# Second attention: two heads per step, with the forget passes and the fp32 scores of both on the two row halves of TensorE

## The reference, cut to what matters

```python
def fox_mixer(xn, w_q, w_o, k, v, c):      # c: cumulative log forget gates, (B, T, H)
    q = (xn @ w_q).reshape(B, T, B_HEADS, HEAD_DIM)
    for i in range(T // BLK):              # BLK = 128
        s = jnp.einsum('bqhd,bkhd->bhqk', q[:, q0:q1], k[:, :q1]) * HEAD_DIM ** -0.5
        s = s + (c_t[:, :, q0:q1, None] - c_t[:, :, None, :q1])
        s = jnp.where(causal, s, NEG)
        p = jax.nn.softmax(s, axis=-1)
        outs.append(jnp.einsum('bhqk,bkhd->bqhd', p, v[:, :q1]))
    return jnp.concatenate(outs, axis=1).reshape(B, T, B_WIDTH) @ w_o
```

## Time and profile before

| | |
|---|---|
| median of 3 runs | 2332.89 us (2332.63 to 2333.86) |
| span of the profiled execution | 2330.7 us |
| TensorE matmul busy | 2212.4 us, 95% of the span |
| second attention, first scores to last values | about 720.1 to 913.6 us |
| of it, with fill between its parts | 720.1 to 893.7 us |

### The profile page before, as it was taken

One profiled execution on the slowest core, in us unless ns is written; L12 is line 12 of the kernel. 1 busy time (PEld: TensorE's weight loads), 2 busy tenths in 40 slices (PEclk: granted clock), 3 DMA queues, 4 the chain that ended last, 5 costly groups with the idle time before them and its releaser, 6 DMA issues.

```text
span 2330.7 us, 34187 instructions
## 1 busy us (share of the span) xinstructions
PE 2212.4 (95%) x14110; PEld 1813.9 (78%) x14110; DVE 1420.4 (61%) x1976; ACT 584.5 (25%) x1199; POOL 1129.2 (48%) x642
## 2 busy tenths in 40 slices
PE   7999899999999999999999998999988978999998
PEld 5877688888877777778788767887888867888886
DVE  6555678667654444667957869687855773721632
ACT  2143322022133222222012132335444222200200
POOL 5711466765744221466666543372400254757654
PEclk9999999999999999999999999999989989999999
DMA  5310223532622110233432551122200111323321
GB/s 176 114 37 19 69 94 118 172 100 92 220 68 68 37 44 21 73 96 109 154 120 98 194 175 37 55 73 74 64 3 3 48 38 55 106 92 99 101 91 63
DMA packets 55769, 201.94 MB, mean 87 GB/s; under 512 B 6560, under 2 KB 6816, under 8 KB 54720
## 3 DMA queue, kind: packets, MB, share of 16 engines
q1 hardware_dynamic: 52272, 187.21, 24.5%
q0 software_dynamic: 1840, 9.60, 1.1%
q10 hardware_dynamic: 1504, 2.95, 0.5%
HBM read 194.76 MB, written 4.19 MB: 85 GB/s over the span
## 4 chain that ended last, share of the span: by engine, by line
PE 86%; DVE 8%; ACT 4%; POOL 1%; issue 1%; DMA 0%; SPq 0%; DVEq 0%; POOLq 0%; ACTq 0%
PE bank L522 65%; PE bank L960 3%; PE bank L988 3%; PE bank L2510 1%; PE bank L975 1%; PE bank L654 1%; PE bank L2774 1%; PE bank L2506 1%; PE bank L964 1%; PE bank L2495 1%; POOL parts_r L503 1%; PE bank L1583 1%; PE bank L1595 1%; PE bank L1395 1%; DVE big L1760 0%
## 5 line engine op out<-in xcount | busy, mean ns | idle before, releaser
L522 PE MATMUL bank<-xn_r,parts_r 128*128 128x512 f32 (+1 forms) x2928 | 917.6, 391 | 32.6 <-DVE mix_r L740 12.7
L522 PE MATMUL bank<-big_r,parts_r 128*128 128x512 f32 x3208 | 929.6, 392 | 2.8 <-POOL parts_r L503 2.4
L497 POOL TENSOR_SCALAR parts_r<-ring 128x1024 fp32r<-128x1024 f32 x293 | 340.0, 1160 | 947.0 <-PE bank L522 936.6
L503 POOL TENSOR_TENSOR parts_r<-ring,parts_r 128x1024 fp32r<-128x1024 f32 x293 | 738.5, 2520 | 24.4
L522 PEld LDWEIGHTS bank<-big_r,parts_r 128*128 128x128 f32 x3208 | 601.3, 189 | 133.5 <-issue 5.6
L522 PEld LDWEIGHTS bank<-xn_r,parts_r 128*128 128x128 f32 x2928 | 553.7, 191 | 151.4 <-issue 27.6
L867 ACT ACTIVATE big<-bank,small 128x512 f32<-128x512 f32 x88 | 68.4, 779 | 411.8 <-DVE big L911 253.1
L896 DVE TENSOR_TENSOR bank<-bank,nb 128x512 f32<-128x512 f32 x88 | 61.3, 699 | 143.5 <-PE bank L522 143.4
L3115 DVE TENSOR_TENSOR big<-big 128x512 f32<-128x512 f32 x32 | 82.7, 2586 | 71.1 <-ACT big_r L3096 71.1
L3041 DVE SCALAR_TENSOR_TENSOR h<-bank,vecs,h 128x512 f32<-128x512 f32 x24 | 17.9, 750 | 173.1 <-PE bank L522 173.1
L533 DVE TENSOR_TENSOR big_r<-big,big_r 128x512 fp32r<-128x512 f32 x76 | 105.7, 1393 | 0.4
(11 more groups left out here) (415 smaller groups left out, 2910.8 us busy)
## 6 DMA issues: line engine op xcount, KB each, us to landing
ring<-weights SPq DMA_DIRECT2D x295, 512.0 KB, 3.5
cst<-mod_w SPq DMA_DIRECT2D x48, 512.0 KB, 3.9
cst<-consts SPq DMA_DIRECT2D x2, 1280.0 KB, 8.4
h<-x SPq DMA_DIRECT2D x8, 256.0 KB, 6.9
h_store<-h POOLq DMA_DIRECT2D x8, 256.0 KB, 2.3
big<-consts POOLq DMA_DIRECT2D x2, 1024.0 KB, 8.2
h<-h_store POOLq DMA_DIRECT2D x1, 2048.0 KB, 9.3
out<-mix SPq DMA_DIRECT2D x8, 256.0 KB, 2.2
```

What stands on the lines that cost most here:

```text
L497: pool.tensor_scalar(rounded(unit_parts(u)[0]), ring[:, u % RING], 1.0, 0.0, ALU.mult, ALU.add)\
L503: pool.tensor_tensor(rounded(lo), ring[:, u % RING], value(hi), ALU.subtract).then_inc(part_ready, 1)
L522: mm = pe.matmul(ps, rounded(w[a]), rounded(x[b]), start=(start and n == 0), stop=(stop and n == 2))
```

## The change

A task now is a pair of heads with a block of queries, 32 in all. TensorE issues the two forget passes first, head 0 on rows 0 to 63 and head 1 on rows 64 to 127, and then both fp32 scores, again on the two halves, into banks 0 and 1. For that `b_sel` and `b_c` hold their rows twice, also 64 partitions higher, and the forget pass has 64 rows instead of 128. Scores run one task ahead instead of two, a piece of fill has two chunks instead of one, and eight chunks are done ahead of the attention instead of six. VectorE writes two more pieces of `b_c`, and takes the third projection before it does. Of a task's two transposes ScalarE copies head 0's and VectorE head 1's. One reciprocal and one `row_out` serve both heads.

```diff
-        sel[h, h] = sel[32 + h, h] = -8.0
+        sel[h, h] = sel[32 + h, h] = sel[HD + h, h] = sel[HD + 32 + h, h] = -8.0
...
-        b_tasks = [(tb, [hd]) for hd in range(B_HEADS) for tb in MIXED]
-        PAIR = 2 * len(MIXED)
+        b_tasks = [(pair, tb) for pair in range(KD) for tb in MIXED]
+        PAIR = len(MIXED)
+        b_S = part(b_work, 4, T).rearrange("p (b g) n -> p b g n", b=2)
...
+        KQ_AHEAD = 2
         def kq_fill(pe, t, half):
-            pair, m = divmod(t + 3, PAIR)
+            pair, m = divmod(t + KQ_AHEAD, PAIR)
             if pair + 1 < KD:
-                kq_part(pe, pair + 1, [(m // 4, 2 * (m % 4) + half)])
+                k = 4 * (m % 2) + 2 * half
+                kq_part(pe, pair + 1, [(m // 2, k), (m // 2, k + 1)])
...
+        def pair_scores(pe, t):
+            pair, tb = b_tasks[t]
+            w = (tb + 1) * P
             if t % PAIR == 0:
+                pe.wait_ge(sem("b_kqt"), 2 * pair + 2)
+            ps = [grab(pe, g, *after("b_masked", 2 * t + g + 1)) for g in range(2)]
+            k_, q_ = kq_slot(0, pair), kq_slot(1, pair)
+            own = slice(tb * P, (tb + 1) * P)
+            for g, r in enumerate(half_rows):
+                pe.matmul(ps[g][:, 0:w], rounded(b_sel[r, 2 * pair + g]), rounded(b_c[r, 0:w]), start=True, stop=False)
+            for g, r in enumerate(half_rows):
+                pe.matmul(ps[g][:, 0:w], b_kq[r, q_, own], b_kq[r, k_, 0:w], start=False, stop=True).then_inc(sem("b_scores"), 1)
...
+        def b_pe(pe):
+            pair_scores(pe, 0)
+            for t in range(b_n + 1):
+                if t + 1 < b_n:
+                    pair_scores(pe, t + 1)
+                kq_fill(pe, t, 0)
+                if t < b_n:
+                    pair_turn(pe, t)
+                kq_fill(pe, t, 1)
+                if t >= 1:
+                    pair_values(pe, t - 1)
...
+        def b_act(act):
+            pair_probs(act, 0)
+            for t in range(b_n):
+                if t + 1 < b_n:
+                    pair_probs(act, t + 1)
+                w = (b_tasks[t][1] + 1) * P
+                act.wait_ge(*after("b_turned", 2 * t + 1))
+                if t >= 2:
+                    act.wait_ge(*after("b_values", t - 1))
+                act.activation(b_PT[t % 2][0][:, 0:w], bank[4][:, 0:w], ACT.Copy).then_inc(sem("b_pt_act"), 1)
...
-            for t in range(-3, 0):
+            for t in range(-KQ_AHEAD, 0):
...
-            for c in range(2):
-                kq_take(dve, c)
+            for i in range(2 + KQ_AHEAD // 2):
+                kq_take(dve, i)
             dve.wait_ge(cst_in, 32)
             c_rows = lambda a, b: rounded(b_c[a:b])
             link(dve, dve.tensor_scalar(c_rows(0, P), cst[:, 0:T], 0.0, None, ALU.mult))
+            dve.tensor_copy(c_rows(HD, HD + B_HEADS), z)
             link(dve, dve.tensor_copy(c_rows(0, B_HEADS), z))
+            dve.tensor_tensor(c_rows(HD + 32, HD + 32 + B_HEADS), z, value(b_c[0:B_HEADS]), ALU.subtract)
             dve.tensor_tensor(c_rows(32, 32 + B_HEADS), z, value(b_c[0:B_HEADS]), ALU.subtract).then_inc(sem("b_c"), 1)
             b_dve(dve)
```

More of the change, by code:

```diff
@@ L338 @@
                ("gd_ss", 3)],
-    "weighted": [("a_values", 16), ("b_values", 64), ("U", 2 * TB), ("gl_o", TB)],
+    "weighted": [("a_values", 16), ("b_values", 32), ("U", 2 * TB), ("gl_o", TB)],
     "rotated": [("conv", 4), ("gl_U", NCH - 1)],
@@ L361 @@
     "pt_dve": [("a_pt_dve", 24), ("b_pt_dve", 32)],
-    "rows": [("a_rows", 16), ("b_rows", 64), ("spec", 2 * TB), ("gl_S", NCH - 1)],
-    "max": [("a_max", 16), ("b_max", 64), ("Y", 2 * TB), ("gl_A", TB)],
+    "rows": [("a_rows", 16), ("b_rows", 32), ("spec", 2 * TB), ("gl_S", NCH - 1)],
+    "max": [("a_max", 16), ("b_max", 32), ("Y", 2 * TB), ("gl_A", TB)],
     "convolved": [("ffn0_conv", 2 * KF), ("ffn1_conv", 2 * KF), ("hy_u", 6), ("gd_conv", 15)],
@@ L935, in build, with attention @@
         MIXED = (0, 2, 3, 1)
-        def attention(st, tasks, G, qT, kT, vT, oT, masks, ring, banks, work, sel=None, due=None, fill=None, take_in=None):
+        def attention(st, tasks, G, qT, kT, vT, oT, masks, ring, banks, work):
             Sb = big[:, work:work + 3 * G * T].rearrange("p (b g n) -> p b g n", b=3, g=G)
@@ L953, in scores @@
                 w = (tb + 1) * P
-                if due:
-                    due(pe, t)
                 for g, hd in enumerate(heads):
@@ L960, in scores @@
                     mm = pe.matmul(ps[:, 0:w], qT[r:r + HD, hd // 2 % ring, tb * P:(tb + 1) * P],
[L961 to L965, removed]
+                                   kT[r:r + HD, hd // 2 % ring, 0:w], start=True, stop=True)
                     mm.then_inc(s("scores"), 1)
@@ L1078, in rows_dve @@
                         row_out(dve, t - 1)
-                    if take_in:
-                        take_in(dve, t)
             return rows_pe, rows_act, rows_dve, n
@@ L1181, in mixa_dve @@
             out_dve(dve, "a", "g01", ("g02", ffn_x, "ffn0_xn"))
-        b_q, b_k = part(0, 2, T), part(2 * T, 2, T)
+        b_kq = part(0, 4, T)
         b_v, b_o = part(4 * T, TB, D), part(4 * T + TB * D, TB, D)
@@ L1187, in build, with kq_slot @@
         b_x, b_xkv = (xn, mix), (part(b_work + 5 * T, KD, T), part(b_work + 5 * T + KD * T, KD, T))
-        b_mask = cst[:, 0:T].rearrange("p (g n) -> p g n", g=1)
+        b_mask = cst[:, 0:T]
         b_sel = cst[:, T:T + B_HEADS * P].rearrange("p (h n) -> p h n", h=B_HEADS)
         b_c = nb[:, 0]
-        b_tasks = [(tb, [hd]) for hd in range(B_HEADS) for tb in MIXED]
-        PAIR = 2 * len(MIXED)
+        b_tasks = [(pair, tb) for pair in range(KD) for tb in MIXED]
+        b_n = len(b_tasks)
+        PAIR = len(MIXED)
         b_oT = (xn, part(0, KD, T))
+        b_S = part(b_work, 4, T).rearrange("p (b g) n -> p b g n", b=2)
+        b_PT = [[big[:, b_work + 4 * T:b_work + 5 * T], nb[:, 1]], [nb[:, 2], nb[:, 3]]]
+        half_rows = [slice(HD * g, HD * (g + 1)) for g in range(2)]
+        def kq_slot(c, pair):
+            return 2 * c + pair % 2
         def kq_part(pe, pair, ks):
@@ L1210, in kq_part, with kq_done @@
                     product_done[u] = after("b_kq", i + 1)
+        KQ_AHEAD = 2
         def kq_fill(pe, t, half):
-            pair, m = divmod(t + 3, PAIR)
+            pair, m = divmod(t + KQ_AHEAD, PAIR)
             if pair + 1 < KD:
-                kq_part(pe, pair + 1, [(m // 4, 2 * (m % 4) + half)])
+                k = 4 * (m % 2) + 2 * half
+                kq_part(pe, pair + 1, [(m // 2, k), (m // 2, k + 1)])
+        def kq_done(t):
+            pair, m = divmod(t + KQ_AHEAD, PAIR)
+            return 2 * (pair + 1) + m // 2 if m % 2 and pair + 1 < KD else None
@@ L1218, in kq_take @@
         def kq_take(dve, i):
+            slot = kq_slot(i % 2, i // 2)
             dve.wait_ge(*after("b_kq", i + 1))
[L1220 to L1228, removed]
-            if t % PAIR == 0:
-                pe.wait_ge(sem("b_kqt"), 2 * (t // PAIR) + 2)
@@ L1232, in build @@
-        b_pe, b_act, b_dve, b_n = attention("b", b_tasks, 1, b_q, b_k, b_v, b_o, b_mask, 2, 2, b_work, sel=(b_sel, b_c),
-                                            due=kq_due, fill=kq_fill, take_in=kq_take_in)
+            if i >= 4:
+                dve.wait_ge(*after("b_scores", 2 * PAIR * (i // 2 - 1)))
+            dve.tensor_tensor(b_kq[:, slot], bank[2 + i % 2][:, :], rstd, ALU.mult).then_inc(sem("b_kqt"), 1)
+        b_stat = lambda t, n: stat[:, 16 * (t % 4) + 2 * n:16 * (t % 4) + 2 * n + 2]
@@ new lines, in pair_turn, with pair_values @@
+        def pair_turn(pe, t):
+            pair, tb = b_tasks[t]
+            for g in range(2):
+                ps = grab(pe, 4 + g, *after("b_pt_dve" if g else "b_pt_act", t + 1))
+                pe.wait_ge(*after("b_probs", 2 * t + g + 1))
+                for kb in range(tb + 1):
+                    mm = pe.transpose(ps[:, kb * P:(kb + 1) * P], b_S[:, t % 2, g, kb * P:(kb + 1) * P], ident)
+                mm.then_inc(sem("b_turned"), 1)
+        def pair_values(pe, t):
+            pair, tb = b_tasks[t]
+            ps = grab(pe, 6 + t % 2, *after("b_rows", t + 1))
+            for g in range(2):
+                pe.wait_ge(*after("b_pt_dve" if g else "b_pt_act", t + 1))
+                for kb in range(tb + 1):
+                    mm = pe.matmul(ps[:, g * HD:(g + 1) * HD], b_PT[t % 2][g][:, kb * P:(kb + 1) * P],
+                                   b_v[:, kb, (2 * pair + g) * HD:(2 * pair + g + 1) * HD], start=(kb == 0), stop=(kb == tb))
+            mm.then_inc(sem("b_values"), 1)
@@ new lines, in b_pe, with pair_probs @@
+        def b_pe(pe):
[9 more added lines that the diff above has]
+                    pair_values(pe, t - 1)
+        def pair_probs(act, t):
+            w = (b_tasks[t][1] + 1) * P
+            act.wait_ge(*after("b_max", t + 1))
+            if t >= 4:
+                act.wait_ge(*after("b_rows", t - 3))
+            for g in range(2):
```

(46 more changed lines are left out.)

4 lines of the change are left out of this document (removed).

## The result

The kernel after takes 2312.99 us in the median of 20 runs, the one before 2333.49 us in 20. The ratio is 0.9919, with a 95% interval of 0.9903 to 0.9935: faster by 19 us (15 to 23), or by 20.5 us if the medians are subtracted. One run in 20 of each kernel, at 2365.8 and 2345.2 us, was slow as a whole (the latter at a mean granted clock of 0.954, the profiled run at 0.972), and the ratio leaves these two out. The forecast was 2310.4, with a range of 2303 to 2320.

What follows compares the result with a forecast made beforehand. The prediction took TensorE's stream to bound the second attention. 31.7 us gained, less 1.9 for the last tasks, 5.8 idle and 1.5 for the clock, gave 22.5: 2332.9 - 22.5 = 2310.4 us, range 2303 to 2320.

Steps and rivals of the forecast that it cites:

- What bounds it: Second attention: TensorE's stream bounds the kernel, busy for all of the 173.6 us that have fill.
- The second head is free: Scores and forget passes: the second head on the other half costs nothing; 3.96 us gained a pair, 31.7 over eight.
- the fixed parts: From score start to fill start in each task: 0.31 us that does not grow with the columns.
- the breaks: Between values and the next scores: some 0.03 us once a task; merging saves 0.12 a pair.
- Strict order: Rival, scores on two halves: MATMULs start first in, first out, costing 8.6 us, so 2319; chance 7%.
- Idle time ahead of the first scores: TensorE waits for b_c behind the third projection and a CAST held by GpSimd: 5.8 us lost.
- The clock: After the idle time ahead of the first scores: about 3 us of work at half speed, 1.5 lost, between 0 and 4.
- The last six tasks: Tasks without fill: waits of 0.2, 0.6 and 1.3 us before transposes, 2.1 in sum, 1.9 lost net.
- with 0.15 for the scaling: Chain from scores to transposes, 512 columns: scaling the maxima counted as 0.15 of about 3.95 us.
- The sum: Whole kernel: 31.7 - 1.9 - 5.8 - 1.5 = 22.5 us gained, giving 2310.4 us.

Runs made afterwards that it cites:

- on one half: Against the kernel after, both heads' forget passes and scores are put on rows 0 to 63: 2333.71 us, ratio 1.0002 to the kernel before.
- head-by-head: Against the kernel after, issue order is forget 0, score 0, forget 1, score 1 instead of both forgets, then both scores: 2312.20 us, ratio 0.9915.
- the later split: Against the kernel after, GpSimd splits the sixth key and query unit only when b_c is written: 2310.92 us, ratio 0.9899.
- the two scalings: Against the kernel after, the scaling of two maxima (128x2) is done as two instructions of 128x1: 2310.66 us, ratio 0.9900.
- all three edits: Against the kernel after: c written before the third projection, scaling as two 128x1, ScalarE's copy ahead of the next exponentials from task 26: 2303.71 us, ratio 0.9859.
- c first: Against the kernel after, VectorE writes c into b_c before it takes the third projection: 2309.80 us, ratio 0.9908.
- extra matmuls: Against the kernel after, TensorE runs twelve extra fp32 matmuls of 256 columns while it waits for b_c: 2310.17 us, ratio 0.9905.

## Why the prediction was right, point by point

- *What bounds it.* Right. The attention ended 21.5 us sooner (913.62 to 892.09, first flip), and TensorE was busy for 145.34 of the 146.10 us that have fill.
- *The second head is free.* Right, and by the stated mechanism: on one half a pair gives back 2.76 of its gain, where 2.7 was the second head's streams, and keeps 1.35, where the fixed parts (4 x 0.31) and the breaks made 1.26. A pair gained 2 x 13.02 - 21.93 = 4.11 us where I had 3.96, 32.9 us over eight pairs instead of 31.7. The forget passes overlap as well, for which no row had stood.
- *Strict order.* The rule of the Trainium skill, "TensorE: Matmul & The Clock Gate", Part 3, "The mechanism", does not hold across halves for the order in which these fp32 and fp32r matmuls start. Line 1544 said so, and the head-by-head order confirmed it (starts 10 ns apart, 21.94 us a pair); the measurement decides.
- *Idle time ahead of the first scores.* Forecast 5.8 us, measured 5.78; first CAST 2.44 us, held by GpSimd, which the later split showed. I had missed 0.69 us more for the second task's scores.
- *The clock.* Forecast 1.5 us for one stretch. The direction was right and the size small: the stretch was 6.8 us long and cost 2.4. The same idle time was followed by 10.2 us of half clock in three other profiles; in the head-by-head one the scores took 8.81 us to the first of 512 columns, so it cost 3.3.
- *The last six tasks.* Forecast 2.1 us of waits, measured 2.94. At tasks 29 and 30 it waited for 0.26 and 1.22, against 0.6 and 1.3 forecast. Task 27 took 1.28 instead of 0.2. The part that was wrong is "with 0.15 for the scaling": I took the 128x1 instruction's time for a 128x2 one, and that one can be held by GpSimd. With fill nothing waits, as forecast, although six more of these scalings took 1.5 us there.
- *The sum.* With measured terms: 32.9 - 2.7 (2.94 less today's 0.2) - 5.8 - 2.4 - 0.7 = 21.3 us, against 21.5 measured at the end of the attention. The forecast of 22.5 was near in part by luck: the gain came out 1.2 us larger than forecast and the losses 2.4 us larger, which offset each other by half.
- *Behind the attention* the profile gave back 2.6 us (21.5 to 18.9). From the first flip to the end the ten profiles last 1413.1 to 1421.3 us although that code is the same in all: 1417.1 before, 1419.7 after. So 2.6 us lies within what this part varies from run to run. That it is a lasting cost was neither shown nor excluded.

## What to carry to other kernels

If two independent matmuls use half of TensorE's rows each, put their operands on different halves and their results in different banks (one bank for both was not tried); a pair then costs what one did, and the order of issue between the halves does not matter. When TensorE's part shrinks, look again at what runs uncovered at both ends of the loop: here an instruction placed ahead of the one that TensorE waits for cost 5.8 us and a clock stretch. Moving it brought the last tasks 8.1 us forward, where the scaling by single columns was worth 1.25; in its profile a half clock at the end took 4.2 of them back. Count a wait near the end of a loop at more than its length: in three of five profiles with the same wait a stretch at half clock followed it.

## What the runs showed of the hardware that was not expected

- VectorE's scaling of two columns (TENSOR_SCALAR, 128x2) took 1.51 to 1.54 us in seven of 32 cases, each beginning inside GpSimd's line 503 and ending with it, and 0.17 us otherwise. On one column it took 0.143 to 0.155 us in all 64 cases, 14 of which began inside line 503. A reciprocal of 128x2 took 0.15 us inside line 503 in the profile of the two scalings, and again in that of all three edits.
- Five kernels have the same last tasks and wait for 1.27 to 1.29 us ahead of task 27's transposes. The profiles of two (the kernel after, and GpSimd's split later) stayed at full clock and took 19.94 us from the scores of task 27 to the first flip; in three (head by head, c first, extra matmuls) the clock fell to half for 6.8, 10.3 and 10.2 us, and they took 3.0, 4.2 and 3.5 us longer. The rows behind the wait with the full and with the half clock:

```profile
874.25 0.66 PE L1253 MATMUL bank<-base,big 128*128 128x128 f32 x4 [1.29 <-ACT big L1297]
874.74 1.00 PE L1262 MATMUL bank<-big 128*128 128x64 f32 x8
```
```profile
884.09 0.66 PE L1250 MATMUL bank<-base,big 128*128 128x128 f32 x4 [1.27 <-ACT big L1294]
884.58 1.66 PE L1259 MATMUL bank<-big 128*128 128x64 f32 x8
```

What decides between the two was not found.
